# Copy marks by bit time in a top-k search, a weight block loaded in two halves, and two copies reordered, in a one-core four-mixer kernel

## What is computed

```python
for l in range(DEPTH):
    h = _rmsnorm(x, norm_g[l])
    p = h @ w_in[l]
    ...
    oc = _dsa(_rope(_heads(cq, C_HEADS), pos), _rope(_heads(ck, C_HEADS), pos), _heads(cv, C_HEADS),
              _rope(_heads(cqi, IDX_HEADS), pos), _rope(cki[:, :, None, :], pos)[:, :, 0, :], cwi) * jax.nn.silu(cz)
    ...
    od = _rwkv7(dr, dk, dv, dwd, dad, ...) * jax.nn.silu(dz)
    y = (sigmoid(ga) * (oa @ w_branch[l, 0]) + sigmoid(gb) * (ob @ w_branch[l, 1])
         + sigmoid(gc) * (oc @ w_branch[l, 2]) + sigmoid(gd) * (od @ w_branch[l, 3]))
    x = x + y @ w_out[l]
return _rmsnorm(x, final_g)
```

## Time and profile before

| | |
|---|---|
| median of 3 executions | 2880.6 us |
| profiled execution, its own time | 2881.09 us |
| its span | 2879.3 us |
| granted TensorE clock, mean of the span | 0.990 |
| busy DVE, ACT, POOL | 55%, 34%, 28% of the span |

### The profile page before, as it was taken

One profiled execution on the slowest core, in us unless ns is written; L12 is line 12 of the kernel. 1 busy time (PEld: TensorE's weight loads), 2 busy tenths in 40 slices (PEclk: granted clock), 3 DMA queues, 4 the chain that ended last, 5 costly groups with the idle time before them and its releaser, 6 DMA issues. The chain is left out here.

```text
span 2879.3 us, 45819 instructions
## 1 busy us (share of the span) xinstructions
PE 2790.9 (97%) x18640; PEld 1493.9 (52%) x18640; DVE 1584.4 (55%) x2979; ACT 967.6 (34%) x1824; POOL 819.7 (28%) x578
## 2 busy tenths in 40 slices
PE   7999999999999999999999899999999999999998
PEld 4436444477644475444444364544776445654443
DVE  2788865633368813065227888656332787130743
ACT  3345764311143335300114457543111433352001
POOL 4323312321144232233052233123211443212330
PEclk9999999999999999999999999999999999999999
DMA  5212101111121221263042111011011212212731
GB/s 211 63 44 59 45 30 45 44 32 32 35 85 34 96 92 48 99 224 112 0 155 58 51 37 44 30 44 44 32 32 50 70 49 93 77 55 92 239 101 59
DMA packets 134985, 204.61 MB, mean 71 GB/s; under 512 B 8920, under 2 KB 88952, under 8 KB 134008
## 3 DMA queue, kind: packets, MB, share of 16 engines
q1 hardware_dynamic: 116184, 167.59, 18.5%
q10 hardware_dynamic: 18592, 34.09, 3.2%
HBM read 146.07 MB, written 48.78 MB: 68 GB/s over the span
## 5 line engine op out<-in xcount | busy, mean ns | idle before, releaser
L474 PE MATMUL ps<-hT,wr 128*128 128x512 f32 x1792 | 830.7, 601 | 3.6 <-ACT wr L528 2.0
L474 PEld LDWEIGHTS ps<-hT,wr 128*128 128x128 f32 x1792 | 326.7, 191 | 371.0 <-issue 354.7
L474 PE MATMUL ps<-sums,wr 128*128 128x512 f32 x896 | 431.3, 610 | 14.0 <-ACT arena L537 13.9
L634 POOL TENSOR_TENSOR gts<-gts,wr 128x512 f32<-128x512 f32 x96 | 138.0, 1437 | 572.0 <-ACT wr L528 349.4
L474 PEld LDWEIGHTS ps<-sums,wr 128*128 128x128 f32 x896 | 164.2, 194 | 192.8 <-issue 168.4
L1102 DVE CUSTOM_DVE_ANT_0 arena<-ps,arena 128x640 f32<-128x640 f32 (+7 forms) x128 | 90.4, 706 | 306.9 <-PE ps L1003 292.7
L713 PE MATMUL ps<-xo,arena 128*128 128x512 f32 x512 | 220.2, 592 | 1.6 <-ACT gts L541 1.6
L528 ACT ACTIVATE wr<-ps 128x512 f32<-128x512 f32 x168 | 99.6, 593 | 358.6 <-PE ps L474 315.4
L474 PE MATMUL ps<-wr 128*128 128x512 f32 x448 | 210.7, 599 | 1.3 <-ACT wr L528 1.3
L1485 DVE TENSOR_SCALAR_CACHE_REDUCE arena<-arena,sm 128x384 f32<-128x384 uint16 (+7 forms) x256 | 192.8, 809 | 2.2
L607 POOL TENSOR_TENSOR wr<-wr 128x512 f32<-128x512 f32 x62 | 84.7, 1365 | 363.6 <-PE ps L474 356.8
(11 more groups left out here) (308 smaller groups left out, 4366.8 us busy)
## 6 DMA issues: line engine op xcount, KB each, us to landing
wr<-in_w_in SPq DMA_DIRECT2D x68, 1024.0 KB, 5.3
gate_tanh<-gts ACTq DMA_DIRECT2D x128, 256.0 KB, 2.1
arena<-gate_tanh SPq DMA_DIRECT2D x128, 256.0 KB, 2.9
x_cur<-arena SPq DMA_DIRECT2D x2, 4096.0 KB, 23.0
arena<-in_w_branch SPq DMA_DIRECT2D x8, 1024.0 KB, 9.9
wr<-in_w_out SPq DMA_DIRECT2D x8, 1024.0 KB, 6.6
arena<-x_cur SPq DMA_DIRECT2D x4, 2048.0 KB, 8.8
arena<-arena SPq DMA_DIRECT2D x36, 128.0 KB, 2.8
```

What stands on the lines that cost most here:

```text
L474: ins = pe.matmul(ap, lhsT=right(u, w_side)[:, kt, :], rhs=left(h_side, kt), start=fresh and kt == 0, stop=kt == half_k - 1, skip_group_ch ...
L634: pool.tensor_tensor(dst, dst, stage_of(u), ALU.add).then_inc(sg("pool_added"), 1)
```

## The change

Seven edits. (1) The marks of ScalarE's copies beside the search: mark 16 ahead of bit 0, and a new formula for bit k; TensorE does 194 steps beside the search. (2) The second weight block of a rows unit is loaded in two halves: the upper one (b11, b12 side) once piece 4 of the unit before is filled, the lower one once piece 5 is; GpSimd waits for the first block and the upper half, makes t1 in two parts, then waits for the lower half and makes t2. (3) At the start of D TensorE does 4 + 4 steps; ScalarE copies what the first four end ahead of the tanh. (4) In the attention (shared by C and A) ScalarE copies the second group of turned probabilities without first copying fills. (5) `select`: the steps are cut at other places. (6) x is loaded tile by tile, in eight loads. (7) The counts of fill steps in D and B change by one here and there.

```diff
--- before.py
+++ after.py
@@ -44,14 +44,14 @@
 IDX_FILL = 1
 A_FILL = 54
 BETWEEN_FILL = 11
-TOPK_FILL = 181
+TOPK_FILL = 194
 ROPE_FILL = 13
 Z_BIT = 22
 PRODUCTS = [("a11", "b11", True), ("a12", "b21", True), ("s2", "t2", False), ("s1", "t1", True), ("s3", "t3", False),
             ("s4", "b22", False), ("a22", "t4", False)]
 FIRST_T = {"t1": 1, "t2": 2, "t3": 3, "t4": 4}
-D_FILL = {"start": 6, "kk": 23, "bonus": 37, "decay": 11, "nat": 2, "AG": 3, "CH": 3, "Y": 1, "X": 2, "UZ": 3, "P": 3, "S": 1, "norm": 12, "turn": 24}
-B_FILL = {"start": 13, "end": (6, 6), "khn": (3, 2), "adds": (3, 3, 3, 13, 1), "att": 1, "last": 2, "turn": 8}
+D_FILL = {"start": 4, "kk": 23, "bonus": 37, "decay": 11, "nat": 3, "AG": 3, "CH": 3, "Y": 1, "X": 2, "UZ": 3, "P": 4, "S": 1, "norm": 13, "turn": 24}
+B_FILL = {"start": 14, "end": (6, 6), "khn": (3, 2), "adds": (3, 3, 3, 13, 1), "att": 1, "last": 2, "turn": 8}
 
 FILL_ORDER = [("D", (0,)), ("C", (0,)), ("C", (1,)), ("D", (4,)), ("C", (4,)), ("C", (5,)), ("C", (2, 3)), ("D", (1,)), ("D", (2,)), ("D", (3,)), ("B", (0,)), ("B", (3,)),
               ("B", (1, 2)), ("A", (0,)), ("A", (3,)), ("A", (1, 2))]
@@ -596,15 +596,18 @@
                 t1, t2, t3, t4 = right(u, "t1"), right(u, "t2"), b12, right(u, "t4")
                 done = 4 * u
                 if 1 in which:
-                    for k in units[u][1]:
+                    k, b11 = units[u][1][0], right(u, "b11")
+                    pool.wait_ge(sg(f"fill_w_loaded{k % 2}"), 16 * (k // 2 + 1))
+                    if is_rows(u):
+                        k0, k, halved = half_k // 2, units[u][1][1], 2 * rows_units(u)
+                        pool.wait_ge(sg("fill_top_loaded"), 16 * (rows_units(u) + 1))
+                        pool.tensor_tensor(t1[:, 0:k0], b12[:, 0:k0], b11[:, 0:k0], ALU.subtract).then_inc(sg("w_half_sums"), 1)
+                        pool.tensor_tensor(t1[:, k0:], b12[:, k0:], b11[:, k0:], ALU.subtract).then_inc(sg("w_sums"), 1)
+                        pool.wait_ge(sg("w_half_sums"), halved + 1)
                         pool.wait_ge(sg(f"fill_w_loaded{k % 2}"), 16 * (k // 2 + 1))
-                    b11, k0 = right(u, "b11"), 0
-                    if is_rows(u):
-                        k0, halved = half_k // 2, 2 * rows_units(u)
-                        pool.tensor_tensor(t1[:, 0:k0], b12[:, 0:k0], b11[:, 0:k0], ALU.subtract).then_inc(sg("w_half_sums"), 1)
-                        pool.wait_ge(sg("w_half_sums"), halved + 1)
                         pool.tensor_tensor(t2[:, 0:k0], b22[:, 0:k0], t1[:, 0:k0], ALU.subtract).then_inc(sg("w_half_sums"), 1)
-                    pool.tensor_tensor(t1[:, k0:], b12[:, k0:], b11[:, k0:], ALU.subtract).then_inc(sg("w_sums"), 1)
+                    else:
+                        pool.tensor_tensor(t1, b12, b11, ALU.subtract).then_inc(sg("w_sums"), 1)
                 if 2 in which:
                     k0 = half_k // 2 if is_rows(u) else 0
                     pool.wait_ge(sg("w_sums"), done + 1)
@@ -835,8 +838,14 @@
             def sp_loads(sp, l):
 
                 loads = [(None, MIX["C"]["sp"])]
+                second = {u[1][1] for u in units if len(u[1]) == 2}
                 for n, (c0, w) in enumerate(fill_blocks):
                     done, sums_of = fill_done[n - 2] if n >= 2 else (None, 0)
+                    if n in second:
+                        top_done = (*done[:3], 4)
+                        loads.append((top_done, wr[:, 2 + n % 2, 0:half_k, 0:w], c0, w, sg("fill_top_loaded"), sums_of, 0))
+                        loads.append((done, wr[:, 2 + n % 2, half_k:, 0:w], c0, w, sg(f"fill_w_loaded{n % 2}"), sums_of, half_k))
+                        continue
                     loads.append((done, wr[:, 2 + n % 2, :, 0:w], c0, w, sg(f"fill_w_loaded{n % 2}"), sums_of))
                 mixer_after = {ORDER[n + 1]: ("oT", ORDER[n], NT - 1) for n in range(3)}
                 for b in ORDER:
@@ -853,12 +862,14 @@
                     if len(load) == 2:
                         load[1](sp, l)
                         continue
-                    key, dst, c0, w, loaded, sums_of = load
+                    key, dst, c0, w, loaded, sums_of = load[:6]
+                    r0 = P * load[6] if len(load) == 7 else 0
+                    r1 = r0 + P * half_k if len(load) == 7 else D
                     if key is not None:
                         jobs.ready(sp, key)
                     if sums_of:
                         sp.wait_ge(sg("w_sums"), 4 * sums_of)
-                    sp.dma_start(dst, w_in[l:l + 1, :, c0:c0 + w].rearrange("l (k p) c -> p (l k) c", p=P)).then_inc(loaded, 16)
+                    sp.dma_start(dst, w_in[l:l + 1, r0:r1, c0:c0 + w].rearrange("l (k p) c -> p (l k) c", p=P)).then_inc(loaded, 16)
 
             def pe_o_turn(pe, b, i, og):
 
@@ -1065,9 +1076,10 @@
                 def act(act):
                     def turned(u, group):
                         g, n = group
-                        ap = act_ready(act, ("PT", b, u, g))
+                        key = ("PT", b, u, g)
+                        ap = jobs.ready(act, key) if g else act_ready(act, key)
                         ins = act.activation(probs_t[u % 3][:, P * g:P * (g + n)], ap[:, 0:P * n], ACT.Copy)
-                        jobs.emptied(ins, ("PT", b, u, g))
+                        jobs.emptied(ins, key)
 
                     for u in range(len(units) + 2):
                         turns = groups(span(u - 1)[3]) if 1 <= u <= len(units) else []
@@ -1226,12 +1238,12 @@
                     if step == 0:
                         link(dve, dve.tensor_scalar(above, sc, v256, None, ALU.is_gt, ALU.add, accum_out=above_count[:, j:j + 1]))
                         link(dve, dve.tensor_scalar(need[:, j:j + 1], above_count[:, j:j + 1], -1.0, float(TOPK), ALU.mult, ALU.add))
+                    elif step == 1:
                         link(dve, dve.tensor_scalar(equal, sc, v256, None, ALU.is_equal))
-                    elif step == 1:
+                    elif step == 2:
                         link(dve, dve.tensor_tensor_scan(sc, equal, equal, 0.0, ALU.add, ALU.max))
-                    elif step == 2:
+                    else:
                         link(dve, dve.scalar_tensor_tensor(equal, sc, need[:, j:j + 1], equal, ALU.is_le, ALU.mult))
-                    else:
                         if j:
                             dve.wait_ge(sg("masks_made"), j)
                         dve.tensor_tensor(chosen, above, equal, ALU.add).then_inc(sg("keys_chosen"), 1)
@@ -1384,10 +1396,10 @@
                     act.wait_ge(sg("index_sums"), 2 * len(index_units))
 
                     def beside(k, half):
-                        passed = 10 + (47 * k) // 10 + 2 * half + 7 * sum(k >= bit for bit in qk_bits) + 8 * (k >= 16)
+                        passed = 18 + (426 * k) // 100 + 2 * half + sum(n for bit, n in ((4, 9), (12, 9), (16, 9), (23, 3), (27, 2)) if k >= bit)
                         act_fills(act, ("beside search", min(passed, searched[0] - 1)))
 
-                    act_fills(act, ("beside search", 12))
+                    act_fills(act, ("beside search", 16))
                     for k in range(32):
                         if k in qk_bits or k == 16:
                             beside(k, -1)
@@ -1796,6 +1808,8 @@
                 def pe(pe):
                     pe_fill_until(pe, ("fills", "D"), ("D", 3))
                     pe_fill(pe, D_FILL["start"])
+                    jobs.mark("before Dw")
+                    pe_fill(pe, 4)
                     pe.wait_ge(sg("wd_tanh"), 1)
                     for what, r0 in (("w", 0), ("a", 64)):
                         for m in range(2):
@@ -1993,6 +2007,7 @@
                     act_fills(act, ("fills", "D"))
                     unit_done(act, ("D", 4))
                     act.activation(z_tanh, z, ACT.Tanh, scale=0.5).then_inc(sg("z_tanh_D"), 1)
+                    act_fills(act, "before Dw")
                     act.wait_ge(sg("wd_shifted"), 1)
                     act.activation(wd[0:64, :], wd[0:64, :], ACT.Tanh).then_inc(sg("wd_tanh"), 1)
                     for n, (what, buf) in enumerate((("w", lw), ("a", a))):
@@ -2243,7 +2258,7 @@
                     eng_name[id(dve)] = "dve"
                     if l == 0:
                         def rows_step(i):
-                            dve.wait_ge(sg(f"x_in{i // 2}"), 16)
+                            dve.wait_ge(sg(f"x_in{i}"), 16)
                             dve.engine_nop().then_inc(sg("rows_in"), 1)
 
                         dve.memset(msq, 1.0).then_inc(sg("root_table"), 1)
@@ -2266,10 +2281,10 @@
                 def _(sp):
                     eng_name[id(sp)] = "sp"
                     if l == 0:
-                        x_pairs = x[0].rearrange("(i p) d -> p i d", p=P)
+                        x_tiles = x[0].rearrange("(i p) d -> p i d", p=P)
                         sp.dma_start(con[:, 0:P], consts[:, 0:P]).then_inc(sg("ident_loaded"), 16)
```

(4 more changed lines are left out.)

## The result

The changed kernel takes 2860.4 us (median of 5 runs, 2859.3 to 2865.1), the kernel before 2880.6: ratio 0.9937, 95% interval 0.9918 to 0.9956. The forecast was 2851.5, so two thirds of the predicted 29.1 us came. The profiled execution took 2859.33 us, its span is 2857.5.

What follows compares the result with a forecast made beforehand. TensorE bounds the kernel: fixed work, plus 88.4 us idle, plus lower clock. 15.5 + 3.2 + 2.3 + 4.0 + 1.2 + 1.7 + 1.2 = 29.1 us off 2881.1, less 0.5 for the median: 2851.5; range 2836 to 2868.

Steps and rivals of the forecast that it cites:

- signs of being wrong: 1.2 GHz beside the search; layer 1's search ending after 356 us, TensorE idle before attention; no 1.2 GHz at D's start.
- the late copies: Beside the search, ScalarE's copies late at the first bits and at pauses: 3.4 us charged for both layers.
- the second rival: Beside the search, TensorE stands 3.66 us after bits 16 and 22, each layer: 14.6, net 12.4 lost, 2863.9; chance 0.14.
- The second way to the same number: Check of edit 1 at C's attention: 11.2 us less at the layer's end; TensorE arrives 1.8 us later, nothing waits.
- the step that failed: C's rows unit, weight block in halves: sums start 2.0 us earlier, waits shrink; 3.2 us won in both layers.
- the other failed step: D's start: products of 64 rows still lower the clock, 10.2 us lost in place of 11.9; 1.7 won, plus 1.2 idle.
- the first rival: At D's start the clock holds once the two waits are gone: 10.2 us more won, 2841.3; chance 0.28.
- the section cited in the prediction: Trainium skill on TensorE's clock: short idle spots between groups cycling through PSUM banks are enough to make the clock swing.
- A's rows unit: In A's rows unit the last of three waits, 1.15 us each, goes with sums 2 us earlier: 2.3 us won.
- The 28 of the prediction: Of 66 fill steps in the closing stretch, 28 leave for search, D and B; 76 instructions there in place of 132.

Runs made afterwards that it cites:

- e1: Changed kernel with VectorE's turning of the queries before bit 8 in place of bit 4; 2855.9 us (0.9912 of before).
- e2: Changed kernel with edit 1 undone (marks and length of the search's fill as before); 2866.8 us.
- e3: Changed kernel with edit 3 undone; 2863.1 us (0.9938 of before).
- e4: Changed kernel without ScalarE's copies ahead of the tanh at D's start, TensorE's steps there kept; 2866.3 us.
- e6: Kernel before with edit 3 alone; 2879.3 us (0.9999 of before).
- e5: Changed kernel with edit 3 undone and two fill steps less at D's start; 2872.1 us.
- e12: e11 with 189 steps of fill beside each search in place of 194; 2842.6 us (0.9882 of before).
- e11: Changed kernel with query turning at bit 8, one piece copied before bits 22 and 26's pauses, x's store before cosines, three more D-decay steps; 2844.6 us.

## Why the prediction was right or wrong

Faster was right, the size was 8.9 us too large, and two errors of about ten each hide in it: C's rows unit came out 9.7 us worse than priced, D's start 11.3 better. They nearly cancel; that 2860.4 lies inside the range of 2836 to 2868, at the edge of the forecast's own 2844 to 2860, is in part luck. Two of the signs of being wrong came: a stretch at 1.2 GHz beside the search, in C's rows unit, and none at D's start.

**Edit 1.** Right: 13.9 of idle and 5.0 of clock went, and the late copies cost 3.7 us more than before (3.4 were charged). They are 2.16 and 1.21 a layer: the first behind the gate of bit 22, which the second rival named, the second after bit 26, which it did not; 6.7 us in all, where it had 14.6. Missed: what TensorE, early, meets next. The step asked only whether the search is over when TensorE reaches the attention (it is: VectorE waits 7.4 us for it), not where TensorE would be when VectorE turns the queries. The second way to the same number failed with it: TensorE comes to the attention 7.4 us later than before in layer 1, not 1.8.

**Edit 2, the step that failed.** "So the first wait falls to about 0.7 us, the second to 0.4" priced each sum at 1.28 us, from a row with no turning beside it, and the text saw that GpSimd "will now sum beside VectorE's turning" and took 0.4 us a layer for that (1.6 in place of 2.0). Four sums at 2.2 in place of 1.28 are 3.7 us. Forecast: 3.2 won. Measured: 8.1 us of waits in both layers, those of the earlier trace rows and their like in layer 2, became 8.7, and about 5.9 of clock behind them are new (the share of the two stretches at 1.2 GHz, half of it lost). e1 and e2 each take the turning away and get the waits down to 1.6 to 2.8 a layer, where the prediction expected 2.5.

The Trainium skill, SBUF — State Buffer, section "SBUF: two separate sides", says that VectorE with two inputs from SBUF and GpSimd hold a shared port one at a time, the other fully blocked. The rows agree in kind: both engines' operations grow at once. In size they do not quite: one of each is done in about 2.2 us, against 1.28 + 1.21 = 2.5 if they only took turns. The bits' counts, with one tensor read, run beside sums of 1.28 in e1. The trace of before had a smaller sign of it that the prediction did not price: two of GpSimd's adds in layer 1 at 1.78 and 1.83 us beside the turning.

**Edit 3, the other failed step.** "What holds the clock down is the kind of product at least as much as the two waits": no. The same sixteen products ran at full clock in both layers of the changed kernel, e3, e4 and e6, eight times without a wait right ahead of or among them, and in the other variants, 24 times in all; the clock fell in three of four places with one, two in the kernel before and one of two in e5. So the first rival's mechanism held, 11.9 us against the 1.7 taken, and 2.3 of idle against 1.2. But the runs say less for edit 3 than that: undone in the changed kernel it makes no difference that can be told (e3), and alone it wins nothing (e6).

The kind of product does count at another place. Ahead of D's decay TensorE does 32 products of 128 rows by 2 columns, with no wait in the 12 us before them. During them or within 2 us behind them the clock fell in 23 of 28 places (fourteen traces, two layers); by half of its stretch a fall cost 1.7 us, or 3.4 where it lasted twice as long. In e12, layer 2, the four fill instructions behind them take 2.81 us, where the four ahead take 1.88:

```profile
1932.91 1.88 PE L474 MATMUL ps<-sums,wr 128*128 128x512 f32 x4
1934.63 3.63 PE L1839 MATMUL ps<-par,arena 128*128 128x2 f32 x32
1938.12 2.81 PE L474 MATMUL ps<-sums,wr 128*128 128x512 f32 x4
```

That TensorE's waits make its clock swing, as the Trainium skill has it in the section cited in the prediction, agrees with D's start but for the second layer of e5, where the wait came and the clock held; the falls at D's products of 2 columns came without a wait.

**Edits 4 and 5.** 4.0 forecast; in C's attention 1.8 us of waits went between the two traces (5.5 to 4.6 a layer). **A's rows unit**: 2.3 forecast, 0.9 came; a wait of 0.65 and 0.83 stays. **Edit 6**: the start moved by 1.23 between the two traces, as forecast 1.2 (the first product comes at 12.5 to 13.4 us in the twelve kernels with the edit, at 13.85 and 14.06 in the two without), but the step stopped there; TensorE's wait at 53 us, behind x's store, gives it back. **Edit 7**: nothing, as forecast, though TensorE waits more than before at D's decay (0.79 a layer) and in D's loop and B (0.1 in layer 1, 3.0 in layer 2). The path was wrong for the steps: a step that a mixer does not take is done ahead of B's turns, and only a whole unit of 28 steps moves to or from the closing stretch. The 28 of the prediction are just that, so its 76 instructions came.

**The sum.** Forecast 29.1. Idle and clock together: search's start 18.9, less 3.7 late in it; rows unit -6.5; D's start 14.2; attention 1.8; A 0.9; x 0.6; decay, loop and B -4.7; a clock stretch near 541 that did not recur, 1.7. That is 23.2, against 21.8 by the spans. The waits in it add up to 10.5, as idle time did. The terms of clock add up to 12.7, and TensorE's busy time fell by 11.3: half of a stretch at 1.2 GHz is a little more than what it cost.

## What to carry to other kernels

Price an operation at its row only if what runs beside it there will run beside it after the change; an edit that shifts one engine by 8 us changes its neighbours. And ask of each gain what the engine arrives at next: time won ahead of a place that another engine times is kept only as far as other work stands there. A clock that fell after a wait in one trace is a chance, not a price: count the places where the same wait left it alone.

## What the runs showed of the hardware

Two operations of 1.2 to 1.3 us on VectorE and GpSimd, each with two tensors as input, both took 2.1 to 2.3 when side by side. The granted clock falls at different places in kernels that are alike around them: TensorE's busy time for the same 18640 instructions lay between 2775.3 (e11) and 2788.2 us (e5) among the variants of the changed kernel, while a difference of 2 to 5 us of idle time is what most single edits here are worth. The same wait of 1.45 us ahead of the same products cost 4.3 us of clock in these products in one layer and nothing in the other. And the clock fell without any wait at 32 products of 2 columns, in 23 of 28 places.
